# Moving two of four gate-row sums over the partitions from TensorE to GpSimd, in a two-layer decoder trunk

## The reference, cut to what matters

```python
def _modulate(c_act, w, b):
    m = (c_act @ w + b)[:, None, :]
    shift, scale, gate = jnp.split(m, 3, axis=-1)
    return shift, scale, gate

for l in range(DEPTH):
    shift, scale, gate = _modulate(c_act, w_ada[l, 0], b_ada[l, 0])
    h = _rms(x, norm_gain[l, 0]) * (1.0 + scale) + shift
    x = x + gate * _hybrid_mixer(h, ...)
    shift, scale, gate = _modulate(c_act, w_ada[l, 1], b_ada[l, 1])
    h = _rms(x, norm_gain[l, 1]) * (1.0 + scale) + shift
    x = x + gate * (_swiglu(h, ...) if l % 2 == 0 else _moe(h, ...))
```

## Time and profile before

| | us |
|---|---|
| three timed runs | 1426.17, 1427.05, 1427.18 (median 1427.05) |
| the profiled execution's own time | 1427.69 |
| its span in the profile | 1426.1 |
| PE busy | 1401.2 (98%) |
| DVE busy | 1228.5 (86%) |
| ACT busy | 901.0 (63%) |
| POOL busy | 51.2 (4%) |

### The profile page before, as it was taken

How to read it: one execution, slowest core, us unless ns; L and a number is a source line. 1 busy time by engine, 2 the same in 40 slices (tenths; PEclk the granted TensorE clock), 3 DMA queues, 4 the chain that set the end, 5 groups by cost and what they waited for, 6 DMA issues and landing times.

```text
span 1426.1 us, 18340 instructions
## 1 busy us (share of the span) xinstructions
PE 1401.2 (98%) x6886; PEld 1136.4 (80%) x6886; DVE 1228.5 (86%) x1077; ACT 901.0 (63%) x800; POOL 51.2 (4%) x91
## 2 busy tenths in 40 slices
PE   5999999999999999999999999999999999999999
PEld 2774899996775888888888888888888888888886
DVE  3679777776887899999999899999899989999987
ACT  3173534342274677777777777777777777777774
POOL 0010000000000000000000000000000000000012
PEclk9999999999999999999999999999999999999999
DMA  9976669779618899999999999999999999999995
GB/s 367 400 318 215 246 226 361 266 271 379 242 57 326 308 370 352 377 393 391 346 397 396 340 396 393 367 370 393 393 342 397 395 341 396 393 372 364 394 391 148
DMA packets 195824, 484.50 MB, mean 340 GB/s; under 512 B 8926, under 2 KB 31684, under 8 KB 191684
## 3 DMA queue, kind: packets, MB, share of 16 engines
q1 hardware_dynamic: 187056, 451.17, 84.5%
q0 software_dynamic: 6480, 32.52, 6.1%
q10 hardware_dynamic: 2244, 0.22, 0.1%
HBM read 473.40 MB, written 10.49 MB: 339 GB/s over the span
## 4 chain that ended last, share of the span: by engine, by line
PE 93%; DVE 3%; DMA 2%; ACT 1%; issue 1%; SPq 0%; DVEq 0%; ACTq 0%
PE ps L1077 21%; PE ps L1079 21%; PE ps L1078 21%; PE ps L889 4%; PE ps L734 4%; PE ps L927 3%; PE ps L926 3%; PE ps L928 2%; DMA arena<-in_w_ada 2%; PE ps L1120 2%; PE ps L727 2%; PE ps L934 1%; PE ps L936 1%; PE ps L935 1%; PE ps L783 1%; PE ps L689 1%
## 5 line engine op out<-in xcount | busy, mean ns | idle before, releaser
L2003 DVE TENSOR_TENSOR split_r<-arena,split_r 128x2048 fp32r<-128x2048 f32 x336 | 763.4, 2288 | 62.2 <-ACT split_r L1408 61.6
L1408 ACT ACTIVATE split_r<-arena 128x2048 fp32r<-128x2048 f32 x334 | 640.2, 1917 | 125.4 <-PE ps L1079 122.1
L1077 PE MATMUL ps<-split_r,tokens_r 128*128 128x512 f32 x1280 | 505.4, 395 | 0.0
L1079 PE MATMUL ps<-split_r,tokens_r 128*128 128x512 f32 x1280 | 499.3, 390 | 0.0
L1078 PE MATMUL ps<-split_r,tokens_r 128*128 128x512 f32 x1280 | 498.3, 389 | 0.0
L1079 PEld LDWEIGHTS ps<-split_r,tokens_r 128*128 128x128 f32 x1280 | 240.2, 188 | 51.2
L1078 PEld LDWEIGHTS ps<-split_r,tokens_r 128*128 128x128 f32 x1280 | 240.6, 188 | 48.0
L1077 PEld LDWEIGHTS ps<-split_r,tokens_r 128*128 128x128 f32 x1280 | 240.4, 188 | 48.0 <-DVE split_r L2003 0.4
L926 PE MATMUL ps<-tokens_r,split_r 128*128 128x256 f32 x352 | 99.2, 282 | 0.2 <-DVE split_r L1843 0.2
L927 PE MATMUL ps<-hT_r,split_r 128*128 128x256 f32 x352 | 99.2, 282 | 0.0
L928 PE MATMUL ps<-tokens_r,split_r 128*128 128x256 f32 x352 | 98.5, 280 | 0.0
(11 more groups left out here) (361 smaller groups left out, 1320.5 us busy)
## 6 DMA issues: line engine op xcount, KB each, us to landing
arena<-in_moe_w_gate SPq DMA_DIRECT2D x57, 2048.0 KB, 10.6
arena<-in_moe_w_up SPq DMA_DIRECT2D x57, 2048.0 KB, 10.9
arena<-in_moe_w_down SPq DMA_DIRECT2D x56, 2048.0 KB, 10.3
arena<-in_w_ada POOLq DMA_DIRECT2D x10, 1536.0 KB, 10.1
arena<-in_w_ada SPq DMA_DIRECT2D x14, 1024.0 KB, 17.3
arena<-in_ffn_w_gate SPq DMA_DIRECT2D x11, 1024.0 KB, 6.6
arena<-in_ffn_w_up SPq DMA_DIRECT2D x11, 1024.0 KB, 13.1
arena<-in_ffn_w_down SPq DMA_DIRECT2D x11, 1024.0 KB, 14.7
```

What stands on the lines that cost most here:

```text
L1077: mm(out_, xh, h, start=first, stop=False, skip_group_check=True)
L1079: return mm(out_, xl, h, start=False, stop=last_, skip_group_check=True)
L1408: A(wh[:, j % SPLITS, :], piece_half(j), ACT.Copy).then_inc(sem("w_hi"), 1)
L2003: v.tensor_tensor(wl[:, j % SPLITS, :], piece_half(j), wh[:, j % SPLITS, :].bitcast(F32), ALU.subtract).then_inc(sem("w_lo"), 1)
```

## The change

The sums for `a` = 0 and `a` = 1 leave PE. `partition_all_reduce` on POOL adds the 128 partitions of a tile and writes the result to all 128.

- `a` = 0: DVE's accumulator is now `first_gate_acc()`, the last 1024 columns of cell 1. The bias comes as one row of 4 KB, and DVE adds it to partition 0 of the accumulator. POOL, after `xr` and ahead of the memset of `blank`, sums 1024 columns into `gate_home(0)`. PE no longer waits for `gate_ok` in layer 0; DVE waits for it ahead of the first `update`.
- `a` = 1: after the third weight transfer of `a` = 2 (k = 2), POOL waits for `gate_ok` 2 and sums the columns in two halves, one into `F`, then one into the first half of `gacc`. PE's two products and ACT's copy are gone; `down_update` reads the two halves.

```diff
+        ffn_gate_rows = (part(F, 2048, 512), gacc[:, 0:512])
-            ("ada", 3, 7, 0, [("grow_ps", 3)]),
+            ("ada", 3, 7, 0, [("grow_ps", 1)]),
+        def first_gate_acc():
+
+            return place(1, CELL)[:, 2 * D:]
-                    sp.dma_start(gate_home(a), b_ada[a // 2, a % 2, 2 * D:].unsqueeze(0).broadcast_to([P, D]))\
-                        .then_inc(sem("bias_in"), 16)
+                    row = b_ada[a // 2, a % 2, 2 * D:].unsqueeze(0)
+                    if a == 0:
+                        sp.dma_start(gate_home(0)[0:1, :], row).then_inc(sem("bias_in"), 16)
+                    else:
+                        sp.dma_start(gate_home(a), row.broadcast_to([P, D])).then_inc(sem("bias_in"), 16)
...
                 if l == 0:
                     pool.wait_ge(sem("xr"), 1)
+                    g.partition_all_reduce(gate_home(0), first_gate_acc(), P, bass.bass_isa.ReduceOp.add)\
+                        .then_inc(sem("gate_ok"), 1)
                     g.memset(blank, 0.0).then_inc(sem("pad"), 1)
...
+                        if k == 2:
+                            pool.wait_ge(sem("gate_ok"), 2)
+                            g.partition_all_reduce(ffn_gate_rows[0], gacc[:, 0:512], P, bass.bass_isa.ReduceOp.add)\
+                                .then_inc(sem("no_outputs"), 1)
+                            pool.wait_ge(sem("no_outputs"), 1)
+                            g.partition_all_reduce(ffn_gate_rows[1], gacc[:, 512:1024], P, bass.bass_isa.ReduceOp.add)\
+                                .then_inc(sem("gate_row"), 1)
...
-                        pe.wait_ge(sem("gate_ok"), 1 + 2 * l)
+                        if l == 1:
+                            pe.wait_ge(sem("gate_ok"), 3)
...
-                    if l == 0 and i == 2:
-                        pe.wait_ge(sem("ada_step"), step["gate", 0, KD - 1])
-                        gate_row_sums(gacc, 2)
...
-                                pe.wait_ge(sem("gate_ok"), 2)
-                                gate_row_sums(gacc, 2)
...
-                act.wait_ge(sem("grow_ps"), 2)
-                A(gacc, bank2(2), ACT.Copy).then_inc(sem("gate_row"), 1)
...
-                        acc = before = gacc
+                        acc = before = gacc if a else first_gate_acc()
...
-                link(v.tensor_tensor(ffn_parts[:, t, half, :], ps[:, 4 + 2 * t + half, :], gacc[:, cols], ALU.mult))
+                link(v.tensor_tensor(ffn_parts[:, t, half, :], ps[:, 4 + 2 * t + half, :], ffn_gate_rows[half], ALU.mult))
...
-                    gate_broadcast(0, 2)
+                    dve.wait_ge(sem("bias_in"), 16)
+                    link(v.tensor_tensor(first_gate_acc()[0:1, :], first_gate_acc()[0:1, :], gate_home(0)[0:1, :], ALU.add))
...
                 rstd(NT, 1.0 / (H * V))
+                if l == 0:
+                    dve.wait_ge(sem("gate_ok"), 1)
```

More of the change, by code:

```diff
@@ L595, in _ @@
                    allow_small_or_imprecise_dtypes=True).then_inc(sem("no_outputs"), 1)
-            pool.wait_ge(sem("no_outputs"), 2)
+            pool.wait_ge(sem("no_outputs"), 3)
             g.memset(mark[:, 3:4], 0.0).then_inc(sem("y_sb"), 1)
@@ L1390, in experts @@
                     A(hnat[:, t, :], bank2(4 + 2 * t), ACT.Copy).then_inc(sem("hnat"), 1)
-                act.wait_ge(sem("grow_ps"), 4)
+                act.wait_ge(sem("grow_ps"), 2)
                 A(gate_row, bank2(0), ACT.Copy).then_inc(sem("gate_row"), 1)
@@ L1576, in gate_broadcast @@
             def gate_broadcast(a, bank):
-                dve.wait_ge(sem("grow_ps"), a + 1)
+                dve.wait_ge(sem("grow_ps"), a // 2)
                 dve.wait_ge(sem("bias_in"), 16 * (a // 2 + 1))
```

## The result

The changed kernel took 1434.32 us, the median of 6 runs (1434.08 to 1435.27), against 1426.82 us before (6 runs, 1425.91 to 1427.66): ratio 1.0053, 95% interval 1.0043 to 1.0063. It is 7.5 us slower, where 3.4 us faster was forecast. The profiled execution took 1434.1 us, span 1432.5 against 1426.1.

A forecast was written before the change was run, and what follows sets the result against it. PE's chain was taken as the bound, PE being busy 98% of the span. Two removed sums of 1.72 us gave 3.44 us removed and 0 added, so 1423.6 us against the 1427.05 median; 8-in-10 range 1422.5 to 1439.

The forecast's parts named there:

- What bounds the kernel: Whole kernel: PE busy 98% of the span, so PE time removed at either sum counts in full unless something else is late.
- Removed, second sum: End of the feed-forward: two PE products leave the path, 1.72 us saved, with modulation, `down_update` and layer 1 moving along.
- Removed, first sum: First mixer's gate: two PE products leave the path, 1.72 us saved, with the instructions next in line having slack.
- The length of a sum: POOL's partition sums: 12 us for 1024 columns and 7 us for 512, assuming groups or trees.
- Where the first sum hides: POOL from `xr` at 93.99 until DVE wants the result at 120.54: cover 26.5 us, no cost up to about 12 us.
- 0 added: Total for POOL's three sums: all hidden, so they add 0 us against 3.44 us removed.
- Rival 1: POOL's sums hold up DVE instructions with two SBUF inputs or at double rate; net +8.8 to +15.9 us, middle 1439, chance 0.24.
- the second place: Feed-forward's two half sums on POOL, 202.9 to 216.9: the DVE-hold rival claimed DVE and PE would feel 8.7 us.
- The prediction's own doubt: Against the DVE-hold rival: an instruction with its own program may let the port go between reads; no size given.
- Rival 2: Sums simply long, 34 us at the high end, delaying DVE, the zeros and k = 3; middle 1438 us, chance 0.11.
- Rival 3: Half the gain taken back: something unmoved (L1238 with the taps, or L1870) follows one removed sum; 1425.3 us, chance 0.13.

The follow-up runs named there:

- the two versions without the hold at this place: Changed kernel with ACT scaling the second and third blocks' row maxima in layer 0, 1423.84 us; or with the first sum behind the third row maximum, 1423.96 us.
- the run with busy PE: Changed kernel with PE repeating four gate products and multiplying the matrix of ones once where its gaps would be; 1427.49 us, ratio 1.0005.
- the one-column sum: Changed kernel with a one-column partition sum ahead to fetch code, and the first sum moved behind the third row maximum; 1423.96 us, ratio 0.998.

## Why the prediction was wrong

**What bounds the kernel** was read rightly for the kernel before: PE's chain. **Removed, second sum: "I count 1.72 us"** was right; the table has -1.73, and alone it measures 1.45 us. **Removed, first sum: "I count 1.72 us"** was too much: the table has -1.06, the timed runs 1.3 to 1.4. The step at fault is "ACT's copy of the recurrent products (L1238) had waited 1.28 us for PE, so it moves up 1.3 of the 1.72 us", with the taps behind it left out of the count. The waits in rows 3 come from a profile in which PE was late by its early clock fall; in the profile of the kernel before with three memsets, which has no such fall, the same copy had waited 0.41 us. That the two versions without the hold at this place measure 1423.84 and 1423.96 us, beside a forecast of 1423.6, hides this, since the kernel before measured 1426.68 beside them and not 1427.05.

**The length of a sum** was taken at 12 and 7 us, inside bounds of 1.5 to 34; it is 6.13 and 3.27. Wrong by a factor of two, on the safe side.

**Where the first sum hides: "So it costs nothing up to about 12 us", in the sum "0 added".** This step failed. I asked only who waits for POOL, and there the cover was ample. L1812 uses the gate at 128.70, 30 us after the sum; the zeros land 12.3 us after their issue at 99.44. I took no account, in the forecast itself, of what DVE is kept from. It cost 3.6 us up to ACT's gates, and this through a DVE instruction of 0.17 us on the way to ACT's exponentials, which feed PE.

**Rival 1** had the mechanism, though not the clock. Its price and its threshold were wrong. It said it "decides from a length of 8 us"; 6.13 us were enough. The 8 us were reckoned to L1761, though the text itself named the small L1737 at 95.39 as perhaps the first held, and that stands 1.4 us behind the sum's start. With its own candidate the threshold would have been that 1.4 us. That the 3.6 us are close to its 3.5 is luck: those were reckoned for L1761, which was not held. It is luck too that 1434.32 lies inside 1422.5 to 1439, a range widened for rivals whose sums are twice as long and in which the clock has no part. Its 8.7 us in the second place were nearly nothing: 0.11 us in the table, although both halves are over its 2.6 us. Each holds DVE for its first 2.1 us only, and these parts fall almost wholly into the 4.84 us that DVE waits for the transfer; L1486 lasts 2.21 instead of 1.82 us:

```profile
216.27 2.21 DVE L1486 TENSOR_SCALAR arena<-arena,cact 128x3072 f32<-128x3072 f32 x1 [4.84 <-DMA arena<-in_w_ada]
```

The Trainium skill ("SBUF — State Buffer", section Who interferes with whom) names the right instructions, two SBUF inputs or a 2-port mode, and these traces agree that reduces from PSUM go free (1.22 us); so do the copies from PSUM. It has the hold last for the whole instruction, and there the traces differ: 4.39 of 6.13 us. By the rule as written the scaling would have ended at 98.4 (92.08 + 6.13 + 0.17) instead of 96.64. The prediction's own doubt, that such an instruction may let the port go in between, was right.

**Missing altogether: the clock.** No step asked what two short gaps of PE do to its granted clock. Of the 10.3 us lost between the end of the taps and the output projection's start (-1.98 to +8.32), 6.7 are this (the fall from 1.00 to 0.50 between 100.4 and 117.5 us). Without it the change would have been level with before, as the run with busy PE shows at 1427.49. **Rival 2** (long sums) had no part. **Rival 3** had a small one: it named L1238 with the taps behind it, and 0.3 to 0.7 of the 3.44 us went there, not half.

Three things stay open: why the clock fell in all 6 runs of the changed kernel but in 6 of 8 with the first sum alone, at the same gaps; why it stayed at half for 17 us there and for 3.4 us in the profile with the later memset; and the 0.3 us between the table's last two rows.

## What to carry to other kernels

Before moving work to GpSimd, list what DVE does beside it: every instruction with two SBUF inputs and every TENSOR_SCALAR on SBUF, the tiniest too, is a candidate for standing still, and what matters is who waits for it. Then see whether the delay opens a gap on TensorE, since a gap can cost more by the clock than by its length. Where the two can't be kept apart in time, moving the small DVE instruction (here to ACT) is as good as moving the big one. And before a wait in a profile is counted as slack, look whether that execution had a clock fall ahead of it.

## What the runs showed of the hardware

- **The hold has two parts.** A TENSOR_TENSOR with two SBUF inputs or a TENSOR_SCALAR that meets the start of the sum is let go 4.38 or 4.39 us after a 1024-column sum begins (six kernels: 96.47 - 92.08 in the changed one, each held instruction's own time taken off) and 2.04 to 2.09 us after a 512-column one. A TENSOR_SCALAR that starts late in the sum (5.11 or 5.72 us in) is held until the sum's end (74.36 and 74.34; 98.52 and 98.50) or that of a memset behind it (99.14 and 99.12). TENSOR_TENSORs with two SBUF inputs are not held there: 0.18 us with the early sum, and 1.22 us for 1024 columns at 100.68 with the later one, as without a neighbour. That the sum reads in the first part and writes in the second is inferred from a memset holding the same kind.
- **A held instruction need not be big.** 128x4 elements waited 3.06 us and 128x6 about 0.9.
- **The first partition sum of a program** stood behind POOL time without a cause in the profile: 11.05 us with the feed-forward's part alone, 6.83 us with busy PE, 5.57 us ahead of the one-column sum. In the changed kernel the wait, 5.84 us, ended with the taps, so nothing shows there. How long it is, and why it varies, is open.
- **The granted clock halves beside gaps of 1.98 and 1.41 us in one execution and not in the next**, and once in a single gap of 2.53 us. Three profiles, of the kernel before among them, have a fall of about 3.5 us between 20 and 36 us; the gaps ahead of it in the profile before (0.51 and 0.72 us the last two) stand in the profile after as well (0.49 and 0.72), without a fall. At half for some 17 us it costs 6 to 9 us here; the early fall made PE 0.9 us late. The mean clock of a profiled run goes with it: 1.0 with no fall, 0.999 with one short fall, 0.998 with two, 0.994 with the long one.
